# Hybrid decoder trunk: the order of the first loads, and where the final norm's scale is applied

## What is computed

```python
def rmsnorm(x, g):
    y = x * lax.rsqrt(jnp.mean(x * x, axis=-1, keepdims=True) + EPS)
    return y * g

mem_k = einsum('bmd,lde->lbme', mem_prompt, w_xa_k)    # 256 memory tokens
mem_v = einsum('bmd,lde->lbme', mem_prompt, w_xa_v)
for l in range(2):
    x = x + mixer_l(rmsnorm(x, norm_mix[l]))           # pooling + conv, then SSM
    x = x + mem_xattn(rmsnorm(x, norm_xa[l]), mem_k[l], mem_v[l])
y = rmsnorm(x, norm_final)
```

## Time and profile before

| | us |
|---|---|
| median of 3 runs | 2480.37 (2478.44 to 2481.13) |
| profiled execution, its own time | 2486.37 |
| span of the profiled execution | 2484.5 |
| TensorE matmul busy | 2327.3 (94%) |
| VectorE / ScalarE / GpSimdE busy | 1308.9 / 605.6 / 654.2 |
| mean granted TensorE clock | 0.975 |

### The profile page before, as it was taken

One profiled execution on the slowest core, in us unless ns is written; L12 is line 12 of the kernel. 1 busy time (PEld: TensorE's weight loads), 2 busy tenths in 40 slices (PEclk: granted clock), 3 DMA queues, 4 the chain that ended last, 5 costly groups with the idle time before them and its releaser, 6 DMA issues. The chain is left out here.

```text
span 2484.5 us, 37348 instructions
## 1 busy us (share of the span) xinstructions
PE 2327.3 (94%) x15121; PEld 2209.6 (89%) x15121; DVE 1308.9 (53%) x2100; ACT 605.6 (24%) x978; POOL 654.2 (26%) x582
## 2 busy tenths in 40 slices
PE   7999999999999988998899999999999997979986
PEld 6999999999999987898798899789879976968985
DVE  4553453332333254556557846883785576435554
ACT  4531100000000033223323312330332133232223
POOL 0023332222222231221123422332343241322220
PEclk9999999999999999999889999999999997999998
DMA  7652222222222234443133323323232332334432
GB/s 219 206 189 96 92 89 85 93 93 93 93 93 93 93 111 155 161 148 125 48 102 106 102 87 105 109 86 113 89 112 85 109 99 70 128 113 159 169 112 89
DMA packets 288070, 280.61 MB, mean 113 GB/s; under 512 B 10634, under 2 KB 251948, under 8 KB 286863
## 3 DMA queue, kind: packets, MB, share of 16 engines
q1 hardware_dynamic: 197592, 124.87, 17.3%
q0 software_dynamic: 24624, 84.42, 9.4%
q10 hardware_dynamic: 65711, 69.32, 8.6%
HBM read 173.48 MB, written 23.73 MB: 79 GB/s over the span
## 5 line engine op out<-in xcount | busy, mean ns | idle before, releaser
L691 POOL TENSOR_TENSOR w_lo<-w_raw,w_hi 128x1024 fp32r<-128x1024 f32 x151 | 382.6, 2534 | 441.9 <-DMA w_hi<-w_raw 441.9
L839 PE MATMUL acc<-h_hi,w_hi 128*128 128x344 f32 x2232 | 489.6, 328 | 9.3 <-DVE h_lo L2056 4.1
L839 PE MATMUL acc<-h_lo,w_hi 128*128 128x344 f32 x2232 | 475.9, 322 | 0.0
L839 PE MATMUL acc<-h_hi,w_lo 128*128 128x344 f32 x2232 | 474.0, 321 | 0.0
L839 PEld LDWEIGHTS acc<-h_hi,w_hi 128*128 128x128 f32 x2232 | 377.0, 190 | 21.5 <-issue 18.2
L839 PEld LDWEIGHTS acc<-h_lo,w_hi 128*128 128x128 f32 x2232 | 379.4, 190 | 0.0
L839 PEld LDWEIGHTS acc<-h_hi,w_lo 128*128 128x128 f32 x2232 | 375.0, 189 | 0.0
L687 POOL TENSOR_TENSOR zero<-zero 128x1 f32<-128x1 f32 x171 | 43.8, 256 | 1088.0 <-issue 663.4
L2016 DVE TENSOR_TENSOR x<-acc,x 128x1032 f32<-128x1032 f32 x96 | 118.3, 1232 | 257.0 <-PE acc L864 257.0
L1046 PE MATMUL acc<-y_hi,w_hi 128*128 128x344 f32 x384 | 128.9, 336 | 14.2 <-DVE x L2200 9.9
L1046 PE MATMUL acc<-y_hi,w_lo 128*128 128x344 f32 x384 | 124.5, 324 | 0.0
(11 more groups left out here) (320 smaller groups left out, 4204.2 us busy)
## 6 DMA issues: line engine op xcount, KB each, us to landing
w_hi<-w_raw POOLq DMA_DIRECT2D x151, 512.0 KB, 2.9
w_raw<-in_w_in_even SPq DMA_DIRECT2D x48, 512.0 KB, 3.7
w_raw<-in_w_in_odd SPq DMA_DIRECT2D x41, 512.0 KB, 3.8
cache<-in_cache_mem_k ACTq DMA_DIRECT2D x8, 2048.0 KB, 9.0
cache<-in_cache_mem_v ACTq DMA_DIRECT2D x8, 2048.0 KB, 8.4
w_raw<-in_w_xa_k SPq DMA_DIRECT2D x16, 512.0 KB, 4.4
w_raw<-in_w_xa_v SPq DMA_DIRECT2D x16, 512.0 KB, 4.1
w_raw<-in_w_out_even SPq DMA_DIRECT2D x16, 512.0 KB, 3.7
```

What stands on the lines that cost most here:

```text
L691: pool.tensor_tensor(lo, raw_ap, hi.bitcast(F32), ALU.subtract).then_inc(done, 1)
L839: ins = pe.matmul(acc[a][:, n * 512:n * 512 + CH], wt[:, s, w], mv[:, k, n * CH:(n + 1) * CH], start=(k == 0 and j == 0), stop=(k == KT - ...
```

## The change

Three parts. (1) SyncE's queue begins with the constants, the memory tiles and the first two weight units; the eight parameter loads follow. The constants have a semaphore of their own, and ScalarE waits for that alone. The parameters are transposed in side job 8, with the sample rows, and kept by two copies. The split of weight unit i stands right behind the eviction of memory tile i. (2) ScalarE's five state transfers are issued in unit 4 of the memory stage, between the `hi_half` and the square. (3) The final norm's scales are no longer spread: tiles are turned unscaled, and VectorE's eviction multiplies each by its token's reciprocal root, a per-partition scalar there, and by the gain row, which is loaded into the free buffer `w_raw[:, 1]`. The sums are taken in two groups: tiles 0 to 4, once the first two thirds are added up, and the rest behind the transposes of tile 2.

```diff
             sp.dma_start(table_in[:, :], ins["constants"]...)
-            (eight loads into p_in, on tables)
+            .then_inc(constants_in, 16)
             for i in range(MT):
                 sp.dma_start(x_in[:, i, :], ins["mem_prompt"][0, i * P:(i + 1) * P, :])...
+            def parameters():
+                (the eight loads into p_in, on tables)
             def x_load(i):
                 if i < 2:
-                    sp.wait_ge(result, i + 2)
+                    sp.wait_ge(result, i + 1)
...
             for u, (l, j, i) in enumerate(MEMORY):
                 columns(ins["w_xa_v" if j else "w_xa_k"][l], i * P)
                 if u == 1:
+                    parameters()
                     x_load(0)
                     x_load(1)
...
+            sp.wait_ge(w_split[GAIN_AT], t.slot[GAIN_AT])
+            sp.dma_start(w_raw[:, GAIN_AT, :], ins["norm_final"]...partition_broadcast(P)...).then_inc(tables, 16)
             for i in range(TT + 1):
                 rows = P if i < TT else NB
                 sp.wait_ge(y_ready, i + 1)
...
 @block.tensor
-            pe.wait_ge(tables, 16 * 9)
             pe.wait_ge(table_r, 2)
-            begin(0)
-            pe.transpose(acc[0][:, 0:112], p_in[0:112, 0, :], ident[0:112, 0:112]).then_inc(w_used[0], 1)
-            pe.transpose(acc[0][:, 112:208], p_in[0:96, 1, :], ident[0:96, 0:96]).then_inc(result, 1)
...
                     pe.wait_ge(x_loaded[n % 2], 16 * (n // 2 + 2))
+                    if n == TT:
+                        pe.wait_ge(tables, 16 * 8)
+                        for k, wide in enumerate(PRM_PARTS):
+                            pe.transpose(turned_in[:, k * P + NB:k * P + NB + wide], p_in[0:wide, k, :], ident[0:wide, 0:wide])
...
-            norm(5)
+            pe.wait_ge(sq_added, added_at[5] + 14)
+            late_sums(range(FIRST))
+            for b in range(NCH):
+                pe.wait_ge(job_out[b], jobs[0] // NCH)
             for i in range(TT + 1):
                 if i < 2:
                     a = begin(i % 2 ^ 1)
-                    pe.wait_ge(fin_ready, KT)
                 else:
                     a, _, _ = t.next(i % 2 ^ 1)
                     pe.wait_ge(y_ready, i - 1)
                 for k in range(KT):
                     ins = pe.transpose(acc[a][0:rows, k * P:(k + 1) * P], x[:, k, i * P:i * P + rows], ident)
+                if i == 2:
+                    pe.wait_ge(sq_added, added_at[5] + 21)
+                    late_sums(range(FIRST, TT + 1))
 @block.scalar
-            (five state transfers)
-            act.wait_ge(tables, 16 * 9)
+            act.wait_ge(constants_in, 16)
             copy(table[:, :], table_in[:, 0:C_INV], table_r)
...
                 copy(m_hi[:, :, i * P:(i + 1) * P], acc[a]..., m_hi_ready)
+                hi_half(i, 1)
...
+                if u == 4:
+                    (five state transfers)
                 if u % 2 == 0 and u // 2 <= TT:
                     square(u // 2)
...
-            norm(5)
-            for i in range(TT + 1):
-                act.activation(y_out[0:rows, i % 4, :], acc[a][0:rows, 0:D], ACT.Copy).then_inc(y_ready, 1)
+            act.activation(sd[:, 0:FIRST], M0[:, 0:FIRST], ACT.Sqrt, bias=eps, scale=1.0 / D).then_inc(root_ready, 1)
+            (the root of the other tiles, behind the second sums)
 @block.vector
-            dve.tensor_copy(prm[:, :], acc[0][:, 0:PRM_N]).then_inc(moved[0], 1)
...
+                if n == TT:
+                    step(dve.tensor_copy(prm[:, 0:PRM_PARTS[0]], turned_in[:, NB:NB + PRM_PARTS[0]]))
+                    step(dve.tensor_copy(prm[:, PRM_PARTS[0]:PRM_N], turned_in[:, P + NB:P + NB + PRM_PARTS[1]]))
...
-            norm(5, PRM_FIN)
+            gain = w_raw[:, GAIN_AT, :]
+            for i in range(TT + 1):
+                if i in (0, FIRST):
+                    dve.reciprocal(rstd[:, tiles], sd[:, tiles]).then_inc(rstd_ready, 1)
+                if i >= 4:
+                    dve.wait_ge(y_stored[i % 4], 16 * (i // 4))
+                dve.scalar_tensor_tensor(out=y_out[0:rows, i % 4, :], in0=acc[a][0:rows, 0:D], scalar=rstd[0:rows, i:i + 1],
+                                         in1=gain[0:rows, :], op0=ALU.mult, op1=ALU.mult).then_inc(y_ready, 1)
```

More of the change, by code:

```diff
@@ L931, in rows_in @@
                     ins = pe.transpose(acc[a][:, k * P:k * P + rows], x_in[0:rows, i, k * P:(k + 1) * P], ident[0:rows, 0:rows])
+                    if i == 0 and k == 0:
+                        ins.then_inc(w_used[0], 1)
                 ins.then_inc(result, 1)
@@ L1376, in _, with late_sums @@
             cross(1, 4, [(s_keep, 11, 8 * i) for i in range(3)])
-            norm(5)
+            def late_sums(tiles):
+                for i in tiles:
+                    rows = P if i < TT else NB
+                    ins = pe.matmul(M0[0:rows, i:i + 1], sum_late[:, i * P:i * P + rows], one, start=True, stop=True)
+                ins.then_inc(summed, 1)
+            pe.wait_ge(sq_added, added_at[5] + 14)
+            late_sums(range(FIRST))
+            for b in range(NCH):
+                pe.wait_ge(job_out[b], jobs[0] // NCH)
             for i in range(TT + 1):
@@ L1901, in _ @@
             cross(1, 4, PRM_XA + KT, waits, conv_rows)
-            norm(5)
-            for i in range(TT + 1):
-                a, r, _ = t.next(i % 2 ^ 1)
-                rows = P if i < TT else NB
-                act.wait_ge(result, r)
-                if i >= 4:
-                    act.wait_ge(y_stored[i % 4], 16 * (i // 4))
-                act.activation(y_out[0:rows, i % 4, :], acc[a][0:rows, 0:D], ACT.Copy).then_inc(y_ready, 1)
+            act.wait_ge(summed, scales_at(5))
+            act.activation(sd[:, 0:FIRST], M0[:, 0:FIRST], ACT.Sqrt, bias=eps, scale=1.0 / D).then_inc(root_ready, 1)
+            act.wait_ge(summed, scales_at(5) + 1)
+            act.activation(sd[:, FIRST:TT], M0[:, FIRST:TT], ACT.Sqrt, bias=eps, scale=1.0 / D).then_inc(root_ready, 1)
+            act.activation(sd[0:NB, TT:TT + 1], M0[0:NB, TT:TT + 1], ACT.Sqrt, bias=eps[0:NB], scale=1.0 / D).then_inc(root_ready, 1)
             act.wait_ge(stored, 16 * (3 + 10))
@@ L1941, in _ @@
                 dve.memset(credit[:, i:i + 1], 0.0).then_inc(s, 1)
-            _, r, _ = t.next(0)
-            dve.wait_ge(result, r)
-            dve.tensor_copy(prm[:, :], acc[0][:, 0:PRM_N]).then_inc(moved[0], 1)
-            dve.wait_ge(moved[0], 2)
             for i in range(MT):
@@ L2036, in scale_tiles @@
             def scale_tiles(n_th, gain, scale_bc):
-                split = n_th < 5
                 for j in range(KT):
-                    if split and j >= 2:
+                    if j >= 2:
                         dve.wait_ge(lo_ready, 8 * (n_th - 1) + j - 1)
-                    ins = dve.scalar_tensor_tensor(out=h32[:, j % 2, :] if split else x[:, j, :], in0=x[:, j, :],
-                                                   scalar=prm_col(gain + j), in1=scale_bc[:, :], op0=ALU.mult, op1=ALU.mult)
-                    if split:
-                        ins.then_inc(h32_ready, 1)
-                        if j:
-                            lo_half(n_th, j - 1)
-                    else:
-                        ins.then_inc(fin_ready, 1)
-                if split:
-                    lo_half(n_th, KT - 1)
-                    dve.wait_ge(lo_ready, 8 * n_th)
+                    dve.scalar_tensor_tensor(out=h32[:, j % 2, :], in0=x[:, j, :], scalar=prm_col(gain + j), in1=scale_bc[:, :],
+                                             op0=ALU.mult, op1=ALU.mult).then_inc(h32_ready, 1)
+                    if j:
+                        lo_half(n_th, j - 1)
+                lo_half(n_th, KT - 1)
+                dve.wait_ge(lo_ready, 8 * n_th)
             def lo_half(n_th, j):
```

60 lines of the change are left out of this document (35 added, 25 removed).

## The result

| | before | after |
|---|---|---|
| median, us | 2479.31 (2473.43 to 2481.13, 5 runs) | 2462.53 (2455.0 to 2464.26, 5 runs) |
| profiled execution, its own time / span | 2486.37 / 2484.5 | 2462.6 / 2460.8 |
| mean granted TensorE clock | 0.975 | 0.979 |

The ratio is 0.9924, with a 95% interval of 0.9910 to 0.9938: 18.8 us faster (15.4 to 22.3). The two medians of the table lie 16.8 us apart, the two profiled executions 23.8. The forecast was 2459.3 us, 21.1 under the kernel before; the measured median is 3.2 us above it.

What follows compares the result with a forecast made beforehand. Bounds: the serial start chain, TensorE's waits in the memory stage up to unit 17, and the end chain through all engines. -5.8 + 2.4 + 0.3 - 18.0 = -21.1 us from the median 2480.37 gives 2459.3, range 2453 to 2466.

Steps and rivals of the forecast that it cites:

- Start, minus 5.8: Start up to the first memory matmul: constants copied at 4.5 us instead of 11.30; minus 5.8 us, between minus 6.8 and minus 1.8.
- The second rival: Start: the parameters were not what held it, constants come late themselves; start only minus 1.8, 2463.3 us; chance 0.13.
- the 1.0 us given back for late first weights: Start: first weights land at 9.6 us while ScalarE wants them at 8.6, giving back 1.0 us.
- State transfers, plus 2.4: Unit 4, memory stage: issuing five transfers delays the square; plus 2.4 us, from 0 to 3.3, nothing added for bytes.
- The argument that the round has no slack: Memory stage: a 7.8 us round runs through the square without slack; TensorE waits 7.3 us in six waits.
- the third rival: Unit 4: the transfer issues on ScalarE cost nothing because the round has slack; 2456.9 us; chance 0.10.
- the parameters' 0.3: Unit 16: two parameter transposes and two copies with the samples; plus 0.3 us, from 0 to 1.2.
- End, minus 18.0: After the last output matmul: spread, copy and scalings leave the path; minus 18.0 us, without any gaps minus 19.7.
- the first rival: End: transposes run at the low clock and TensorE becomes the bound, 3.5 us later; 2462.8 us; chance 0.12.
- The constant offset: Whole kernel: the profiled execution's 6.0 us above the median of the runs carries over, so 2465.3 profiled means 2459.3.
- Slower: Loop of loads: transfers cost 4.4 us a round; with six such rounds plus 5.3, 2485.7 us; chance 0.02.

Runs made afterwards that it cites:

- Run 10: Kernel before with the new end and the state transfers out of the loop of loads, start still waiting for all parameters: 2458.95 us, ratio 0.9913.
- Run 3: Changed kernel with the five state transfers back at the head of ScalarE's queue, ahead of the copy of the constants: 2457.36 us, ratio 0.9914.
- run 12: Changed kernel with the five state transfers in unit 4 cut to 8 columns each, issues unchanged: 2458.76 us, ratio 0.9911.
- run 5: Changed kernel with state transfers out of the loop of loads (two in unit 17, three behind the memory stage): 2455.99 us, ratio 0.9900.
- run 9: Changed kernel with state transfers out of the loop of loads and the second column sums behind tile 1: 2454.24 us, ratio 0.9892.
- run 11: Kernel before with the new start, the old end, and the state transfers out of the loop of loads: 2475.67 us, ratio 0.9979.
- run 4: Changed kernel with the five state transfers issued by GpSimd behind the weight split of unit 4, not by ScalarE: 2457.18 us, ratio 0.9915.
- run 1: Kernel before with the new end alone (sums by tile, scale and gain at the eviction), old start: 2463.77 us, ratio 0.9933.
- run 2: Kernel before with the new start alone, state transfers in unit 4, old end: 2477.05 us, ratio 0.9993.
- run 8: Changed kernel with the second column sums behind tile 1 and nine output buffers: 2460.31 us, ratio 0.9919.
- run 6: Changed kernel with the eight parameter loads back ahead of the memory tiles, ScalarE waiting for the constants alone: 2463.14 us, ratio 0.9934.

## Why the prediction was right

The sign and the size of the gain were as argued, and nearly all of it lies at the end, as forecast; the sum of 21.1 us lies within the measured 15.4 to 22.3. The share of the start came out right by luck, as shown below. By the prediction's own steps:

- **Start, minus 5.8.** Minus 6.9 at the first memory matmul, just past the end of its range: the copy was at 4.18 us (4.5 forecast), and the 1.0 us given back for late first weights did not come, they were in time. The assumed 1.3 us from the constants to the first memory tile rests on no row; it measured 1.4 (4.18 to 5.57). The second rival, constants that come late themselves, is out by the 4.18. But the reading behind it was only half right. The row before names the last parameter load as what ScalarE waited for the earlier trace rows, and I took the wait for the cause. Run 10 keeps the wait and takes the five state transfers away: 5.87 us. Run 3 takes the wait away and keeps the transfers: 7.11 us, and 19.00 for the first memory matmul. The parameters were late because the five transfers went beside them: 1.25 MB, as the 1.38 of the earlier trace rows hold a store of 128 KB that is none of the five. The change did both, so the number held.
- **State transfers, plus 2.4.** The step that failed in size: "I add nothing for them in the sum", said of the bytes. The delay of the square was 2.4 us to the tenth, and the issues alone (run 12 against runs 5, 9, 11) cost 2.3 at the end of the stage. With the bytes it was 5.4 (144.6 against 139.2), beyond the upper end of 3.3. Most of the bytes did travel while SyncE's queue was empty, as argued: ScalarE's queue moved 0.90 MB from 36 to 39 us. But 0.29 MB more followed from 39 to 41.5, beside the token tile issued at 39.01; unit 8's weights behind it landed 2.5 us late, and the low clock came on top. The argument that the round has no slack also counted a wait too many: of the 7.3 us that TensorE waits in six waits, 3.7 end at 20.09 us, ahead of the loop, so the loop's own waits up to 70 us are 3.6 us in five. The Trainium skill, page "DMA: Bandwidth & Descriptors", section "Issuing engines are not separate DMA queues", says that transfers of different issuing engines run on the same 16 DMA engines and interleave; run 4 agrees (unit 8 at 50.53 us with ScalarE's queue empty). It also says that issue time is usually small beside the transfer, and here the first issue takes 0.64 us for a transfer that lands 4.2 us after it. But small is not free: the five stand in ScalarE's program ahead of the square and hold it up by 2.4 us. So the third rival is out, by the square and by the 2.3 us of run 12.
- **Start and transfers together.** Minus 3.1 in the sum with the parameters' 0.3, minus 3.2 measured at the last scaling (147.8 to 144.6). It fits because the gain without transfers is 8.6 us (139.2), not 5.8, and their cost 5.4, not 2.4. Two errors of 3 us cancelled: that is luck. From 21 to 150 us TensorE waits for split weights 5.7 and 4.2 us in the kernel before and run 1, and 2.5, 4.4 and 2.8 in runs 5, 9 and 11: 1.7 less in the mean, which with the 6.9 at the first matmul makes the 8.6. With the transfers in unit 4 it is 5.4 to 8.2. In the time itself the start with its transfers is not clear of noise (run 2). The 0.3 for the parameters was not measured by itself.
- **End, minus 18.0.** Minus 17.5 (37.3 to 19.8), and 17.3 in run 1. Evictions of 1.28 us and the store wait (0.79 for 0.9) came as costed; the gaps at tiles 3 and 4 were 1.28 and 0.41 instead of 0.6 in all, and 0.43 where the clock held. So the first rival was true for some 3 us and no longer: the clock fell to 0.50 and came back to 1.00 between 2450 and 2454, with transposes alone on TensorE. The Trainium skill, page "TensorE: Matmul & The Clock Gate", section "Part 4: PE-mode transpose", says that the full clock does not engage for TensorE's transpose mode; for the fp32 tiles turned here (whether in that mode no row says) these windows disagree, as the earlier trace rows did. What the prediction did not see is the bound behind it: run 8 shows that the stores leave nothing to win from more buffers.
- **The constant offset.** "Which I take as a constant offset" failed. The 6 us by which the profiled execution of before lay above its median are no property of profiling: the change's profiled execution, 2462.6 us, is at its median (with the offset it should have been 2465.3), and other executions of the kernel before went up to 2489.33. The spread comes from the stretch between the two marks, which varied by 11 us over fourteen profiles. Between its shortest (run 4) and its longest (run 9) TensorE's busy time differs by 2.8 us and its idle time by 8.1. The idle time is spread over waits for VectorE's results (`o_lo` 6.6 and 9.1 us, `dec` 1.6 and 3.5, `dta` 1.8 and 3.3, `x` 1.4 and 2.7). Why these waits differ from run to run stays open.
- **Slower.** It needed six rounds with 4.4 us lost in each; one round lost 4.9 (the lead fell from 7.9 to 3.0).

## What to carry to other kernels

The transfer that a wait names need not be the cause of its length: look at what else is in flight, and test by moving that away. A head start is worth what is left at the next mark that the edit does not touch; here 6.9 us were 3 after 130 us, because transfers moved out of one critical chain into another, and behind the loop of loads the same transfers cost 5 us less at that mark and 3 to 8 us less by the ratios. In a tail that hands tiles from engine to engine, put small extra work into the waits that are there, and count the bytes still to be stored: here the last 10 us are theirs.

## What was not expected of the hardware

A wait of TensorE was followed by several busy microseconds at half clock: after the wait for unit 8 it was busy without a break from 50 to 54 us at 0.50, and got through 23 matmuls; in run 5, at 1.00, it was 20 in 2 us from 46 to 50. The same happened after waits of 1.5 us in the end, in some profiles of the same code and not in others (clock 0.50 in the change and in runs 1, 5 and 6, 1.00 in runs 3, 4, 10 and 12), which by itself moved the end by 1 us. And the final stores ran at 389 to 422 GB/s with the DMA engines full, while the loop of loads, whose rounds wait for each other, moved 185 to 243 GB/s from 18 to 58 us in the kernel before, and still lost 5 us to the issues and the 1.25 MB of five more transfers.
